# The requests for the 64 value pages: from GpSimd's queue to SyncE's

## What is computed

```python
proj = h @ w_in                                   # input projection, 12 column groups of 512
k_past = cache_k[l][page_table].reshape(dec_b, -1, SB_HEADS, SB_HEAD_DIM)   # 8 samples x 8 pages
v_past = cache_v[l][page_table].reshape(dec_b, -1, SB_HEADS, SB_HEAD_DIM)
z = einsum('bhqd,bhkd->bhqk', q, k) * scale + bias
a = exp(log_sigmoid(z) + tail_sums(log_sigmoid(-z)))     # stick-breaking weights
o = einsum('bhqk,bhkd->bhqd', a, v)
out = concat([o_sb, o_gla]) @ w_out               # then the feed-forward network
```

## Time and profile before

| | us |
|---|---|
| three runs | 1499.48, 1501.0, 1501.34 |
| median | 1501.0 |
| span of the profiled execution | 1497.3 |
| PE busy in the span | 1440.9 (96%) |
| time to landing of a value page (38 that are named v_page) | 7.9 |
| time to landing of a key page | 8.0 |

### The profile page before, as it was taken

The page is one execution under the profiler, slowest core; times in us unless marked ns, Lnnn a source line. Parts: engine busy times, 40 slices in busy tenths (PEclk is TensorE's granted clock), DMA queues, the critical chain, the costliest instruction groups (busy, mean ns, idle before and its releaser), DMA issues.

```text
span 1497.3 us, 29248 instructions
## 1 busy us (share of the span) xinstructions
PE 1440.9 (96%) x11262; PEld 1275.6 (85%) x11262; DVE 921.3 (62%) x1517; ACT 665.8 (44%) x1303; POOL 104.5 (7%) x205
## 2 busy tenths in 40 slices
PE   7869999999899999998999999999999999999997
PEld 2237787887678787796899999999999999999997
DVE  2234588996677666368756666566665675446444
ACT  1023477677565544444543434434344343334333
POOL 1000311113322200000000000000000000200000
PEclk9879999999899999999999999999999999999999
DMA  9989999999999979985766566665656655855552
GB/s 368 419 332 361 391 391 406 372 328 400 397 398 324 337 262 346 397 329 215 263 184 179 168 188 181 182 182 167 188 178 182 182 168 189 234 180 182 181 177 93
DMA packets 139331, 396.82 MB, mean 265 GB/s; under 512 B 13163, under 2 KB 17682, under 8 KB 126434
## 3 DMA queue, kind: packets, MB, share of 16 engines
q1 hardware_dynamic: 118018, 319.66, 62.9%
q0 software_dynamic: 21232, 76.10, 13.3%
HBM read 382.28 MB, written 11.34 MB: 263 GB/s over the span
## 4 chain that ended last, share of the span: by engine, by line
PE 84%; DMA 10%; DVE 3%; ACT 1%; issue 1%; POOLq 0%; POOL 0%; SPq 0%; DVEq 0%; ACTq 0%
PE ps L1988 24%; PE ps L1989 23%; PE ps L1990 23%; PE ps L1922 5%; DMA ada_s<-in_w_ada 3%; DMA v_page<-in_cache_v 2%; DMA k_page<-in_cache_k 2%; PE ps L2120 1%; DMA ada_r<-in_w_ada 1%; PE ps L2046 1%; DMA raw<-in_w_ffn_gate 1%; PE ps L1965 1%; DMA k_page<-in_cache_v 1%; DVE w_lo L1271 1%; ACT k_page L813 0%
## 5 line engine op out<-in xcount | busy, mean ns | idle before, releaser
L1988 PE MATMUL ps<-h_hi,w_hi 128*128 128x264 f32 x2304 | 667.1, 290 | 9.8 <-DVE h_lo L1259 3.6
L1989 PE MATMUL ps<-h_lo,w_hi 128*128 128x264 f32 x2304 | 657.9, 286 | 0.0
L1990 PE MATMUL ps<-h_hi,w_lo 128*128 128x264 f32 x2304 | 657.5, 285 | 0.0
L1988 PEld LDWEIGHTS ps<-h_hi,w_hi 128*128 128x128 f32 x2304 | 437.3, 190 | 56.1 <-issue 36.1
L1813 DVE TENSOR_TENSOR w_lo<-raw,w_hi 128x1024 fp32r<-128x1024 f32 x254 | 307.2, 1214 | 273.1 <-ACT w_hi L1057 271.7
L1057 ACT ACTIVATE w_hi<-raw 128x1024 fp32r<-128x1024 f32 x264 | 278.5, 1059 | 408.2 <-PE ps L1990 388.3
L1989 PEld LDWEIGHTS ps<-h_lo,w_hi 128*128 128x128 f32 x2304 | 436.7, 190 | 0.1
L1990 PEld LDWEIGHTS ps<-h_hi,w_lo 128*128 128x128 f32 x2304 | 435.6, 189 | 0.0
L1271 DVE TENSOR_TENSOR w_lo<-raw,w_hi 128x1024 fp32r<-128x1024 f32 x138 | 168.6, 1223 | 144.6 <-ACT w_hi L725 144.1
L725 ACT ACTIVATE w_hi<-raw 128x1024 fp32r<-128x1024 f32 x128 | 135.1, 1056 | 176.7 <-PE ps L1990 147.1
L1989 PE MATMUL ps<-act_lo,w_hi 128*128 (+1 forms) x704 | 200.4, 285 | 0.0
(11 more groups left out here) (363 smaller groups left out, 1224.9 us busy)
## 6 DMA issues: line engine op xcount, KB each, us to landing
ada_r<-in_w_ada SPq DMA_DIRECT2D x64, 1024.0 KB, 9.6
raw<-in_w_in SPq DMA_DIRECT2D x96, 512.0 KB, 8.4
raw<-in_w_ffn_gate SPq DMA_DIRECT2D x88, 512.0 KB, 3.7
raw<-in_w_ffn_up SPq DMA_DIRECT2D x88, 512.0 KB, 3.8
raw<-in_w_ffn_down SPq DMA_DIRECT2D x88, 512.0 KB, 4.5
ada_s<-in_w_ada SPq DMA_DIRECT2D x32, 1024.0 KB, 12.9
k_page<-in_cache_k POOLq DMA_DIRECT2D x64, 512.0 KB, 8.0
v_page<-in_cache_v POOLq DMA_DIRECT2D x38, 512.0 KB, 7.9
```

The lines of the kernel that those rows point to most:

```text
L1988: mm(out, w_hi, xh, start=first, stop=False)
L1989: mm(out, w_hi, xl, start=False, stop=False)
L1990: return mm(out, w_lo, xh, start=False, stop=last)
```

## The change

GpSimd no longer requests value pages. SyncE does, in its loop over slots: the pages that `page_values` of slot t frees are requested at s = t + 4, behind the weight request of that s. Pages 0 and 1 stand at s = 55, pages 2 and 3 at s = 59, page 4 at s = 62. The waits in front of each page are the same ones, now made by SyncE; places, semaphores, page sizes and everything on PE, ACT and DVE stay.

```diff
             for s in range(2, NSLOT - 4):
                 sp.wait_ge(lo_ready, s + 1)
                 w_load(s + 4)
+                if s in (55, 59):
+                    v_page(s // 2 - 27)
+                    v_page(s // 2 - 26)
+                if s == 62:
+                    v_page(4)
+                if s - 4 in AV_AT:
+                    for m in (2 * AV_AT[s - 4] + 5, 2 * AV_AT[s - 4] + 6):
+                        if m < TS * PAGES:
+                            v_page(m)
...
             for s in range(20, 97):
-                if s == 58:
-
-                    v_page(4)
                 for n in range(5, TS * PAGES):
                     if s == KP_SLOT[n - 5] + (n - 5) % 2:
                         k_page(n)
-                if s in (53, 55):
-                    v_page(s - 53)
-                    v_page(s - 52)
...
-                if s in AV_AT:
-                    for m in (2 * AV_AT[s] + 5, 2 * AV_AT[s] + 6):
-                        if m < TS * PAGES:
-                            v_page(m)
```

`v_page` itself moves with its waits and is the same but for the engine:

```diff
-                    pool.wait_ge(av_used, (m - 5) // 2 + 1)
+                    sp.wait_ge(av_used, (m - 5) // 2 + 1)
...
-                page = pool.value_load(PT[0:1, m:m + 1], min_val=0, max_val=NPOOL - 1)
-                pool.dma_start((VPA if m < 32 else VPB)[m % 5][:, :],
+                page = sp.value_load(PT[0:1, m:m + 1], min_val=0, max_val=NPOOL - 1)
+                sp.dma_start((VPA if m < 32 else VPB)[m % 5][:, :],
```

More of the change, by code:

```diff
@@ L435, in state_load, with v_page @@
                     .then_inc(state_in[c % 3], 16)
+            def v_page(m):
+                if m in (0, 1):
+                    sp.wait_ge(kft_tr, 1)
+                elif m == 2:
+                    sp.wait_ge(g_st, 1)
+                elif m == 3:
+                    sp.wait_ge(vg_tr, 4)
+                    sp.wait_ge(vsmp_ready, 1)
+                elif m == 4:
+                    sp.wait_ge(g_o, GH)
+                else:
+                    sp.wait_ge(av_used, (m - 5) // 2 + 1)
+                if m == 32:
+                    sp.wait_ge(k_even, 32)
+                    sp.wait_ge(k_odd, 32)
+                page = sp.value_load(PT[0:1, m:m + 1], min_val=0, max_val=NPOOL - 1)
+                sp.dma_start((VPA if m < 32 else VPB)[m % 5][:, :],
+                               pool_v[bass.ds(page, 1), :, :].rearrange("o p n -> p (o n)")).then_inc(vpage_in[m % 5], 16)
             for s in range(2, NSLOT - 4):
```

15 lines of the change are left out of this document (removed).

## The result

| | before | after |
|---|---|---|
| median of 4 runs | 1500.92 us | 1506.38 us (1504.34 to 1509.36) |
| profiled execution, span | 1497.3 us | 1502.7 us |
| ratio, 95% interval | | 1.0047 [1.0034, 1.0061] |

The forecast was "within 0.2%". The time lies outside that, on the slow side, and just inside the range (its end was 1506.5 us). The ratio on record isn't the quotient of the two medians: it is 1.0047, that is 7.1 us, where the medians are 5.5 us apart (1.0036).

The account below looks back on a forecast made before the run. PE sets the end, and its waits for value pages lie in a stage bound by DMA bytes. Terms 0 + 0 + 0 + 0 - 0.5 gave -0.5 us: 1500.5 against 1501.0 us, range 1495.5 to 1506.5.

Parts of the forecast that it names:

- within 0.2%: Whole kernel: the change makes no difference that can be measured, within 3 us; chance 0.44.
- full stage: 340 to 440 us, DMA engines full at 398 GB/s: rate may rise slightly, -0.5 us, ends -5 and 0.
- GpSimd's key pages sooner: Two key pages after page 8, freed from GpSimd's value-page wait, go some 7.7 us sooner; DVE's 4.05 us wait goes.
- The pair of waits: Wait at page_values(2) grows by 2.6 us, most of 4.14 at page_values(4) goes; 0 together, ends -1.5 and +2.6.
- SyncE's request: SyncE's 64 added page requests cost 1.0 us each, covered by its own waiting; weights don't get late, 0 us.
- The later request: SyncE must see the low half first, so pages are requested later: +1.0 us; as a slower rival 1504.5, chance 0.09.
- The shorter path: Value pages land faster by SyncE's queue than by GpSimd's: -1.0 us, cancelling the later request.
- the store that I took as the far end: 16 KB on GpSimd's queue taking 6.0 us, used as upper bound for that queue's fixed landing time.
- The second stage: 460 to 550 us: only one 0.36 us wait for value pages there, so gains at most 0.4 us; taken as 0.
- lost turns: Full stage: value pages fall behind weights and states in SyncE's queue, +4.5 us, 1505.5; chance 0.19.

Follow-up runs that it names:

- e13: Changed kernel with the 64 value pages requested by ScalarE on its own queue, behind its high half: 1525.15 us, 1.0175.
- e5: Changed kernel with GpSimd making all its old value-page waits but requesting none, so key pages go late as before: 1505.05 us, 1.0046.
- e2: Kernel before, with pages still on GpSimd's queue but GpSimd also waiting for the low half that SyncE waits for: 1502.23 us, 1.0018.
- e8: e1 with value pages 7 and 8 moved behind page 4: 1496.84 us, 0.9994.
- e1: Changed kernel with SyncE requesting all value pages one slot sooner: 1501.02 us, 1.0015.
- e7: Changed kernel with value pages requested ahead of the weights of the same slot, behind the same low half: 1499.64 us, 1.0009.
- e14: e7 run a second time, on the chip of e13: 1501.29 us, 1.0017.
- e9: e8 with pages 0 to 3 also requested ahead of their slot's weights: 1502.18 us, 1.0021.
- e11: e10 with the first three state blocks requested one slot later: 1500.88 us, 1.0012.
- e12: Changed kernel with only the first three state blocks requested one slot later: 1504.9 us, 1.0049.
- e10: e7 with page 4 requested one slot sooner and ahead of pages 7 and 8: 1502.47 us, 1.0028.
- e15: e8 run a second time, on the chip of e13: 1499.23 us, 1.0007.
- e0: Changed kernel with no edit, timed again: 1504.52 us, 1.0038.

## Why the prediction was wrong

The step that failed is the **full stage**: "the stage is bound by bytes, and who asks for them doesn't change the bytes", with -0.5 us and ends -5 and 0 for the rate. The bytes didn't change; the rate did, 398 to 382 GB/s, +4.2 us. The argument looked only upward (is there room above 398?) and took 398 as given. A full stage stays full only while somebody asks in time. The changed kernel at 382 and, the second time, 373 GB/s, and e13 at 371, show how easily that ends. The end above zero was missing from this term, though the rival had it.

Point by point:

- **GpSimd's key pages sooner: right, and worth nothing.** Predicted about 361.7 and 362.9 us:

```profile
361.37 0.53 POOL L611 DMA_DIRECT2D k_page<-in_cache_k  x1 [6.18 <-ACT k_page L812]
362.53 0.53 POOL L611 DMA_DIRECT2D k_page<-in_cache_k  x1 [0.63 <-issue]
```

  DVE's waits for key pages between 340 and 450 us fell from 11.5 to 2.2 us, the one of 4.05 went. e5 shows that it doesn't move the time.
- **The pair of waits: right in kind at page_values(4), wrong in place otherwise.** Most of the 4.14 us went there (1.81 left). Predicted was 3.4 us at page_values(2); it waits 0 (page 4 lands in 4.6 us, at 378.3), and page_values(1) waits 5.92. I had costed only page 4 against two key pages on the other queue, and not pages 2 and 3 against the weights on their own. The rows for it were in the trace of before: page 3 at 9.9 us and the weights of that slot at 13.2.
- **SyncE's request: right.** 1.0 us per page was taken; two requests follow each other by 1.13 us (383.12, 384.25), the issue itself is 0.36. SyncE still waits for DVE 50.1 us, and 9.6 us now for value steps, in three waits, 8.3 at most. The weights behind the longest weren't late by it, since their low half needed the same value step.
- **The later request: right in size, wrong in its price.** In slot 82 of the changed kernel:

```profile
497.42 1.04 PE L2119 MATMUL ps<-k_page,a_dec 128*32 128x512 f32 x8
...
498.22 1.23 DVE L1270 TENSOR_TENSOR w_lo<-raw,w_hi 128x1024 fp32r<-128x1024 f32 x1 [0.93 <-ACT w_hi L724]
499.48 0.39 SPq L400 DMA_DIRECT2D raw<-in_w_in  x1
500.63 0.34 SPq L453 DMA_DIRECT2D k_page<-in_cache_v  x1
```

  The request stands 2.17 us behind the end of the value step, where it stood 1.23: 0.94 later, +1.0 predicted. But it was netted against the shorter path to zero. e2 prices the moment at 2.7 us (3.5 by the medians), and all of it lies ahead of page_values(15): behind it e2's stage is as long as before, 95.0 us.
- **The shorter path: not shown.** Median landing in the second stage (pages 37 to 63) fell from 6.88 to 6.42 us, 0.46 and not 1.0. But in e2, on GpSimd's queue with the late moment, it is 5.93: a later request alone lands sooner by more than that. And e5, with the same requests on SyncE's queue, has 5.82, so kernels that share a queue differ by as much. So neither the -1.0 nor the 0.46 can be put down to the path; the store that I took as the far end did not resemble a page. The Trainium skill ("DMA: Bandwidth & Descriptors", Latency and other measured facts) has about 0.6 and 1 us to the first byte, an estimate of 0.4 us for the path; no run here isolates it. In the full stage the path isn't shorter but longer, as page 3 shows.
- **The second stage: right.** page_values(15) to (31) is 95.7 us, before 95.0. A page there is 1.1 us later asked for and 0.5 faster, and has the room.
- **The rival that came near: lost turns**, priced at 1505.5 us. Its row was the right one: packets of 3.6 KB on one queue against 1.6 on the other. Its place was wrong: it was to decide by page 4, landing after 378.7 us, and page_values(4); page 4 was just in time, and it decided by page 3 and page_values(1). And it named only one of two causes. What spoke against it, that "the queue is in the order in which PE needs its pages", doesn't hold. Weights have four slots to spare, and stand ahead of pages; and among the pages, page 4, which page_values(2) wants, stands behind 7 and 8, which page_values(3) and (4) want. e8 against e1 shows what that order is worth when the requests come early: 1.0015 against 0.9994 and 1.0007.

How much is place and how much moment? By the ratios the late moment on GpSimd's queue costs 2.7 us (e2 against before) and the changed kernel 5.7 to 7.1; by the medians it is 3.5 against 5.5 to 6.4. So some 2 to 4 are left for the place. From the other side, e7 and e14 give back 2 to 6 us by order within the slot, and the earliest moment (e1) about 3 to 5. The two overlap and the parts don't add exactly, since every change of order also moves the requests behind it. What stays open: why e9 is slower than e8 (SyncE's long stand in front of page 2 is a candidate that no run tests), and whether the later state blocks help in e11, as they don't in e12. Both are within 2 to 4 us, and each trace shows only that another page had become the late one.

No variant beats the kernel before; e8_page4 can't be told from it.

## What to carry to other kernels

A stage that runs at the DMA limit is bound by bytes only while its requests come in time, so a change of requester in it isn't free by itself: look for the loss of rate that a late piece can cause, not only for the gain. Before moving an urgent transfer to another queue, list what is queued there at that moment and how long that takes to land; an urgent piece behind one that has four slots to spare has changed places with it. But a request that must wait for its place holds up all that stand behind it, 12.2 us in e10, so moving it forward is no gain by itself either; and look at what else the move passes, as `ada_r` in e1 and e8. And a large wait in a full stage is a place where the shortage shows, not its cause: e1, e8, e10, e11 and e12 each shortened one wait and found one of about 5 us or more again at a later value step.

## What the runs showed of the hardware

- A page of 0.5 MB takes 3.5 to 16.3 us to land in this stage (e1's page 9, e15's page 11; 6.1 to 11.5 in the kernel before), by what stands ahead of it. The moment of the issue says little about the moment of the landing.
- At about 352 us the same page took 12.7 us on SyncE's queue (13.4 in e0) and 9.1 on ScalarE's, and on GpSimd's 9.9, or 9.0 in e2. ScalarE's requests appear as a queue of their own in the profile (q10, 33.56 MB, the 64 pages), and SyncE's stay in q1.
- Around a long wait of PE the granted clock is down to 1.2 of 2.4 GHz: in the changed kernel for 6.8 us from 361.6 on, where PE stood 5.9 us until 363.7, and the value step that ran in it took 1.93 us instead of 1.06. The value steps behind e12's and e10's waits of 5 us took as long (1.93, 1.94), with the granted clock at 1.2 GHz from 396.6 and from 389.0 us on.
- A request on SyncE with a page number costs 1.13 us, on GpSimd 1.16. The cheaper issue (0.36 against 0.53) is nearly used up by what stands in front of it, the reading of the number above all (0.77 against 0.63).
